# Gate rows by way of DRAM, one norm's row from an input, and x kept by the weights' queue, in a two-block transformer kernel

## The chip, the cores and the metric

The kernel runs on one core of a Trainium2 chip as one program. The metric is the device time of that program in microseconds. Its engines are named here as the profile does: PE is TensorE (PEld its weight loads), DVE VectorE, ACT ScalarE, POOL GpSimd, SP SyncE; SPq, POOLq and ACTq are the issuing of DMAs on those queues. The result must equal the reference in float32.

## What is computed

The reference runs two blocks of depth 2 on 256 tokens of width 1024. What touches the change:

```python
def rmsnorm(x, g):
    x32 = x.astype(jnp.float32)
    y = x32 * lax.rsqrt(jnp.mean(x32 * x32, axis=-1, keepdims=True) + EPS)
    return (y * g.astype(jnp.float32)).astype(x.dtype)
...
def first_block(x, c, ...):
    c_act = jax.nn.silu(c)
    for l in range(DEPTH):
        mod = c_act @ mod_w[l] + mod_b[l]
        sh1, sc1, g1, sh2, sc2, g2 = jnp.split(mod, 6, axis=-1)
        h = modulate(x, norm_g[l, 0], sh1, sc1)
        ...
        x = x + (g1[:, None, :] * y).astype(x.dtype)
        h = modulate(x, norm_g[l, 1], sh2, sc2)
        y = peer(h, peer_w_q[l], peer_subkeys[l], peer_u[l], peer_v[l])
        x = x + (g2[:, None, :] * y).astype(x.dtype)
        ...
    return rmsnorm(x, final_norm_g)

def second_block(x, c, ...):
    for layer in range(DEPTH):
        sh1, sc1, g1, sh2, sc2, g2 = jnp.split(c_act @ mod_w[layer] + mod_b[layer], 6, axis=-1)
        ...
        x = x + g1[:, None, :] * rms_norm(y, norm_g[layer, 1])
        h = modulate_2(rms_norm(x, norm_g[layer, 2]), sh2, sc2)
        y = sq_relu_mlp(h, ffn_w1[layer], ffn_w2[layer])
        x = x + g2[:, None, :] * rms_norm(y, norm_g[layer, 3])
    return x
```

`g2` is a vector of 1024 that multiplies every token's output, so on the chip it is wanted as a row repeated on all 128 partitions. `final_norm_g` is such a vector too.

## The kernel before

**Stages.** Block 1 runs a GLA mixer, PEER layer 0, sliding-window attention, PEER layer 1 and the final norm (`fin`). Block 2 runs an mLSTM mixer, FFN 0 (`f2_0`), MLA, and FFN 1 (`f2_1`). Tokens are two tiles of 128 (`NT`), the width eight chunks of 128 (`DC`) or two halves of 512.

**Weights.** A product in float32 is made of three products of halves: hi by hi, hi by lo, lo by hi. SP streams all weights as slabs of 1 MB into `ring`, two slabs deep, each slab in two transfers of 512 KB (L3198 for the first two slabs of a stage, L3214 in the loops, L3231 for the rest). ACT rounds a slab to its hi part (L1559), DVE makes the lo part (L1606), and PE multiplies. Before it loads into a half of `ring`, SP waits until that half's lo part is made.

**PEER.** A layer has a query stage (`peer_q`, L1459), scores of all 16384 experts (the u stage, 64 slabs), and the value loop (64 slabs, L2088, 24 products of 512 columns a slab). Between them GpSimd adds the chosen experts' weights into `routes` in DRAM by 128 indirect transfers (L1582). `routes` is cleared by SP in pieces of 1 MB (L3176); for layer 0 the last two pieces are issued behind the first and second slab of `peer_q0`.

**x kept.** The score inputs `h_parts` lie over the same memory as `x`. So GpSimd stores x to DRAM (`x_kept`, L3256, four transfers of 256 KB, each as soon as DVE has made that piece). In `peer_score_scalar` ACT waits for all four landings before `chunk_scalar` (L1025) writes `h_parts`. Near the end of the value loop GpSimd loads x back as `kept` (L3267, two transfers of 512 KB), for the residual.

**Gate rows.** modulation vectors are made as columns, `[128, 8]`, by DVE (`chunk_product`, L372) from strips that GpSimd loads: `first_mod_loads` before PEER layer 0, `strip_loads_gpsimd` (L411) in the value loops, `side_loads_gpsimd` (L452, four slots, each load waiting until the chunk four before it has been used) in the rest. `row_from_col` turns a column into a row on all partitions: DVE multiplies `ident` by the column (L473), and PE multiplies `ones` by the result into two PSUM banks (L484). `row_store` copies the banks to `row` (L492, DVE). `gated_vector` (L921) multiplies a stage's output by `row`. In each value loop the g2 row's products stand between slab 55 and 56, and in layer 1 those of the final norm's gain (`fin`) at slab 60. In the FFNs they stand behind the first step of the second matrix (`post_tensor`), and DVE copies them in `post_rest_vector`, behind the last split.

**Dummies.** `keep_busy_tensor` (L997) gives PE products of `ident` by itself, as many as the table `KEEP_BUSY` says, where it would wait; `pq0` is the place before the queries of PEER layer 0.

**Order.** The order of each engine is the order of the code; there is no planner. The queues are SP's (weights, clears), GpSimd's (strips, x kept, rows of c) and ACT's (routes' groups).

## Time and profile before

| | us |
|---|---|
| median of three runs | 2526.43 |
| the three runs | 2525.45, 2526.43, 2528.55 |
| the profiled execution's own time | 2524.33 |
| its span | 2522.6 |
| PE busy | 2448.2 (97%) |
| DVE busy | 2042.9 (81%) |
| ACT busy | 1266.6 (50%) |
| POOL busy | 672.4 (27%) |
| mean granted clock of TensorE | 0.989 |
| moved by DMA | 572.51 MB, mean 227 GB/s |

The span is from the first to the last instruction of the profiled execution; 1.7 us lie outside it. "Busy" is the share of the span in which an engine runs at least one instruction. A row of the timeline gives its start, how long it (or the group of like instructions) took, the engine and the line, the destination and the sources, and in brackets the idle time before it with what ended that.

### The profile page before, as it was taken

The page shows a single profiled execution, that of the slowest core. Times are in us where ns is not written, and L with a number is a line of the kernel's source. Part 1 is how long each engine was busy: PE and PEld are TensorE (multiplying, and loading weights), DVE is VectorE, ACT ScalarE, POOL GpSimd, SP SyncE. Part 2 cuts the span into 40 slices and gives each one's busy share as a digit, 9 for nine tenths or more (in the row PEclk, how much of TensorE's full clock was granted, in tenths as well). Part 3 has the DMA queues.
Part 4 walks back from the last instruction along what each step waited for, and adds up shares of the span by engine and source line. Part 5 has one row for each costly group of instructions (what it writes and reads, how often), then busy time and mean ns, then how long its engine had stood idle before and what let it go on. Part 6 is the DMA issues. An engine that isn't in the chain of part 4 may idle for free.

```text
span 2522.6 us, 41648 instructions
## 1 busy us (share of the span) xinstructions
PE 2448.2 (97%) x14618; PEld 2109.6 (84%) x14618; DVE 2042.9 (81%) x3772; ACT 1266.6 (50%) x1825; POOL 672.4 (27%) x548
## 2 busy tenths in 40 slices
PE   5999999999999999999999999999999999999998
PEld 4779988888888877899988888887878799867987
DVE  7888899888778888869999787778887887777754
ACT  5544555655444445445555555444454544334443
POOL 2113777772000001017777750001011000110000
PEclk8999999999999999999999999999999999999999
DMA  9976877776667987366777766668977567863554
GB/s 351 353 266 235 266 187 191 187 173 219 203 209 253 307 291 272 124 225 168 184 193 190 177 182 228 205 207 310 312 266 266 214 206 263 320 245 122 180 179 150
DMA packets 226199, 572.51 MB, mean 227 GB/s; under 512 B 55777, under 2 KB 86753, under 8 KB 225778
## 3 DMA queue, kind: packets, MB, share of 16 engines
q1 hardware_dynamic: 122674, 431.56, 50.6%
q0 software_dynamic: 70000, 120.43, 17.9%
q10 hardware_dynamic: 33360, 18.36, 2.4%
q8 instruction: 98, 1.61, 0.3%
q14 instruction: 67, 0.55, 0.1%
HBM read 550.20 MB, written 20.06 MB: 226 GB/s over the span
## 4 chain that ended last, share of the span: by engine, by line
PE 83%; DVE 9%; DMA 4%; ACT 3%; issue 2%; SPq 0%; POOL 0%; DVEq 0%; ACTq 0%; POOLq 0%
PE ps L2088 26%; PE ps L1526 14%; PE ps L1530 7%; PE ps L2829 7%; PE ps L744 6%; PE ps L1459 5%; PE ps L2811 5%; PE ps L1507 4%; PE ps L2815 2%; PE ps L1511 2%; DMA ring<-in_stream 2%; PE ps L1815 1%; ACT split_hi L1559 1%; DVE split_lo L1606 1%; DVE gate L921 1%
## 5 line engine op out<-in xcount | busy, mean ns | idle before, releaser
L1559 ACT ACTIVATE split_hi<-ring 128x1024 fp32r<-128x1024 f32 x760 | 800.6, 1056 | 678.0 <-PE ps L1530 222.5
L1606 DVE TENSOR_TENSOR split_lo<-ring,split_hi 128x1024 fp32r<-128x1024 f32 x676 | 823.4, 1219 | 177.8 <-ACT split_hi L1559 171.8
L1582 POOL DMA_INDIRECT routes<-small x256 | 478.1, 1868 | 162.4 <-issue 93.3
L1526 PE MATMUL ps<-h_parts,split_hi 128*128 128x512 f32 x1536 | 387.2, 394 | 0.2
L1526 PEld LDWEIGHTS ps<-h_parts,split_hi 128*128 128x128 f32 x1536 | 275.8, 189 | 49.9 <-issue 0.9
L1556 ACT ACTIVATE gate_hi<-gate 128x256 fp32r<-128x256 f32 x252 | 105.2, 418 | 369.1 <-PE ps L2088 357.6
L2088 PE MATMUL ps<-split_hi,gate_hi 128*128 128x512 f32 x1024 | 281.0, 394 | 2.1 <-DVE gate_lo L1604 1.3
L2088 PE MATMUL ps<-split_hi,gate_lo 128*128 128x512 f32 x1024 | 277.0, 390 | 4.6 <-DVE gate_lo L1604 4.4
L2088 PE MATMUL ps<-split_lo,gate_hi 128*128 128x512 f32 x1024 | 277.8, 391 | 0.0
L2088 PEld LDWEIGHTS ps<-split_hi,gate_lo 128*128 128x128 f32 x1024 | 191.4, 188 | 48.1 <-DVE gate_lo L1604 7.6
L2088 PEld LDWEIGHTS ps<-split_lo,gate_hi 128*128 128x128 f32 x1024 | 191.0, 188 | 44.9 <-DVE split_lo L1606 5.2
L2088 PEld LDWEIGHTS ps<-split_hi,gate_hi 128*128 128x128 f32 x1024 | 189.2, 188 | 43.1 <-ACT split_hi L1559 3.5
L1530 PEld LDWEIGHTS ps<-h_parts,split_lo 128*128 128x128 f32 x1536 | 209.2, 190 | 16.8 <-DVE split_lo L1606 2.1
L1530 PE MATMUL ps<-h_parts,split_lo 128*128 128x256 f32 x1536 | 214.4, 282 | 0.7 <-DVE split_lo L1606 0.7
L1604 DVE TENSOR_TENSOR gate_lo<-gate,gate_hi 128x256 fp32r<-128x256 f32 x252 | 106.4, 422 | 132.0 <-ACT split_hi L1559 131.9
L411 POOL DMA_DIRECT2D mod_w<-in_mod x64 | 34.0, 532 | 659.5 <-DVE strip_part L372 659.5
L452 POOL DMA_DIRECT2D small<-in_mod x104 | 55.2, 531 | 488.1 <-DVE modc L372 461.0
L372 DVE CUSTOM_DVE_ANT_0 small<-small,gate,cols 128x1024 f32<-128x1024 f32 x104 | 131.8, 1279 | 5.5 <-DMA small<-in_mod 5.5
L1507 PE MATMUL ps<-h_parts,split_hi 128*128 128x256 f32 x1024 | 133.7, 283 | 0.7 <-ACT split_hi L1559 0.6
L1507 PEld LDWEIGHTS ps<-h_parts,split_hi 128*128 128x128 f32 x1024 | 127.4, 192 | 1.2 <-ACT split_hi L1559 1.1
L2964 DVE TENSOR_TENSOR split_lo<-ring,split_hi 128x1024 fp32r<-128x1024 f32 x60 | 73.3, 1222 | 31.2 <-ACT split_hi L1559 31.2
L372 DVE CUSTOM_DVE_ANT_0 mod_w<-mod_w,c_loop 128x1024 f32<-128x1024 f32 x64 | 78.0, 1219 | 11.2 <-DMA mod_w<-in_mod 11.2
(412 smaller groups left out, 3739.2 us busy)
## 6 DMA issues: line engine op xcount, KB each, us to landing
ring<-in_stream SPq DMA_DIRECT2D x776, 512.0 KB, 4.8
small<-in_mod POOLq DMA_DIRECT2D x104, 512.0 KB, 5.9
mod_w<-in_mod POOLq DMA_DIRECT2D x64, 512.0 KB, 5.7
gate<-in_mod POOLq DMA_DIRECT2D x44, 512.0 KB, 6.9
routes<-u_part SPq DMA_DIRECT2D x16, 1024.0 KB, 12.8
small<-routes ACTq DMA_DIRECT2D x120, 128.0 KB, 5.4
gate<-in_mod SPq DMA_DIRECT2D x8, 512.0 KB, 16.1
routes<-small POOLq DMA_INDIRECT x256
```

Source lines behind the costliest of these rows:

```text
L372: return nc.vector.tensor_tensor_reduce(out=w, in0=w, in1=c_act, scale=1.0, scalar=start, op0=ALU.mult, op1=ALU.add, accum_out=out)
L744: return nc.tensor.matmul(ps[:, banks[2 * nb + i], :], src[:, b * per + n, i * P:(i + 1) * P], w[:, b % 2, at_:at_ + BANK], start=(b == n ...
L1459: ins = nc.tensor.matmul(out, w[:, b % 2, c * P:(c + 1) * P], src[:, c, :], start=(c == 0 and w is split_hi and src is hi), stop=(c == DC ...
L1507: nc.tensor.matmul(out, split_hi[:, e, c * P:(c + 1) * P], part[:, c, :], start=(part is hT_hi and c == 0), stop=False)
L1526: nc.tensor.matmul(ps[:, bank, :].rearrange("p (a n) -> p a n", a=2), split_hi[:, e, c * P:(c + 1) * P], h_parts[:, :, c, :], start=(c == ...
L1530: ins = nc.tensor.matmul(ps[:, bank, SEQ:2 * SEQ], split_lo[:, e, c * P:(c + 1) * P], hT_hi[:, c, :], start=False, stop=(c == DC - 1), ski ...
L1559: nc.scalar.activation(split_hi[:, e, :], ring[:, slot, e * D:(e + 1) * D], ACT.Copy).then_inc(hi_made, 1)
L1582: g.eng.indirect_dma_start(out=routes, out_offset=bass.IndirectOffsetOnAxis(ap=r_index[:, b, n:n + 1].bitcast(U32), axis=0), in_=r_weight[ ...
L1606: nc.vector.tensor_tensor(split_lo[:, e, :], ring[:, (START[name] + j) % RING, e * D:(e + 1) * D], split_hi[:, e, :].bitcast(F32), ALU.sub ...
L2088: return nc.tensor.matmul(ps[:, 2 * nb + n, :], g[:, e, n * P:(n + 1) * P], w[:, e, nb * BANK:(nb + 1) * BANK], start=opens, stop=True, sk ...
L2811: nc.tensor.matmul(out, split_hi[:, e, c * P:(c + 1) * P], part[:, c, :], start=(part is mlp_hi and c == 0), stop=False)
L2829: return nc.tensor.matmul(ps[:, 4 + 2 * nb + n, :], h[:, c0, n * P:(n + 1) * P], w[:, e, nb * BANK:(nb + 1) * BANK], start=(first and h is ...
```

## The change

Five of the rows are no longer made by products. For `g2_0`, `g2_1`, `f2_0` and `f2_1` GpSimd stores the column to DRAM (`gate_row_store`) and loads it back with the same 1024 values on every partition (`gate_row_load`). DVE waits for that landing in front of the residual. The row of `fin` is loaded in the same way from a new input. The rows of the mixers' gates are made as before.

GpSimd issues the g2 store behind the indirect adds, in front of the loads of the value loop's strips, and the row's load (in layer 1 also that of `fin`) behind the two loads of `kept`. In FFN 0 the store stands between side chunks 3 and 4, where GpSimd waits for the gain column, and the load in front of side chunk 7. For FFN 1 both stand behind all side loads.

The stores of x to `x_kept` go from GpSimd's queue to SP's, behind the first two slabs of `peer_q0` and `peer_q1` and, in layer 0, behind the two clears. `KEEP_BUSY["pq0"]` goes from 12 to 2.

SP at the start of PEER layer 0 before (L3198 are the halves of `peer_q0`'s first two slabs, L3176 the clears, L3214 the slab loop):

```order
L3198 DMA ring<-in_stream 128x1024 x2
L3176 DMA routes<-u_part 512x1x512
L3198 DMA ring<-in_stream 128x1024 x2
L3176 DMA routes<-u_part 512x1x512
L3226 UNCONDITIONAL_BRANCH
L3226 ISA
L3214 ISA
L3214 DMA ring<-in_stream 128x1024
```

and now:

```order
L3204 DMA ring<-in_stream 128x1024 x2
L3182 DMA routes<-u_part 512x1x512
L3204 DMA ring<-in_stream 128x1024 x2
L3182 DMA routes<-u_part 512x1x512
L3217 DMA x_kept<-x 128x512 x4
L3238 UNCONDITIONAL_BRANCH
L3238 ISA
L3226 ISA
L3226 DMA ring<-in_stream 128x1024
```

The four stores of x stand behind the second clear on SP's queue.

GpSimd from the end of the value loop of layer 0 to the strips of layer 1's before (L3267 is `kept`, L334 the next block's or stage's row of c, L452 the side chunks, L3256 x kept, L1569 the first splits of the u stage, L1582 the indirect adds, L1590 the first groups of routes):

```order
L3267 DMA gate<-x_kept 128x1024 x2
L334 DMA gate<-c_kept 128x1024
L452 DMA small<-in_mod 128x1024 x16
L3256 DMA x_kept<-x 128x512 x4
L452 DMA small<-in_mod 128x1024 x8
L1569 TENSOR_TENSOR split_lo<-ring,split_hi 128x1024 x12
L1582 DMA routes<-small 2097152x1 x128
L1590 DMA small<-routes 128x2x128 x4
L337 DMA c_loop<-c_kept 128x1024
```

and now (L507 is the row's load, L501 the column's store):

```order
L3280 DMA gate<-x_kept 128x1024 x2
L507 DMA gate<-gate_rows 128x1024
L336 DMA gate<-c_kept 128x1024
L456 DMA small<-in_mod 128x1024 x24
L1586 TENSOR_TENSOR split_lo<-ring,split_hi 128x1024 x12
L1599 DMA routes<-small 2097152x1 x128
L1607 DMA small<-routes 128x2x128 x4
L501 DMA gate_rows<-modc 128x8x1
L339 DMA c_loop<-c_kept 128x1024
```

The row's load stands behind `kept`, the column's store behind the indirect adds, and the side chunks no longer have the stores of x among them.

PE at the end of the value loop of layer 0 before:

```order
L2088 MATMUL ps<-split_lo,gate_hi 128x512 x4
L2117 REGISTER_ALU
L2117 COMPARE_AND_BRANCH
L484 MATMUL ps<-gate,ones 128x512 x2
L2088 MATMUL ps<-split_hi,gate_hi 128x512 x4
L2088 MATMUL ps<-split_hi,gate_lo 128x512 x4
```

and now:

```order
L2092 MATMUL ps<-split_lo,gate_hi 128x512 x4
L2121 REGISTER_ALU
L2121 COMPARE_AND_BRANCH
L2092 MATMUL ps<-split_hi,gate_hi 128x512 x4
L2092 MATMUL ps<-split_hi,gate_lo 128x512 x4
```

The two products of ones behind the loop's branch are gone.

The diff, cut:

```diff
         x_kept, x_back = sem("x_kept"), sem("x_back")
+        gate_row_stored, gate_row_landed, fin_row_landed = sem("gate_row_stored"), sem("gate_row_landed"), sem("fin_row_landed")
+        GATE_ROWS = ["g2_0", "g2_1", "f2_0", "f2_1"]
         sems = {"V": vector_steps, "A": scalar_steps, "T": tensor_steps, "G": gpsimd_steps, "S": slab_used, "L": lo_free}
...
-        def side_loads_gpsimd(g, stage, first=0, last=None):
-
-            for s in SIDE_STRIPS[stage][first:last]:
+        def side_loads_gpsimd(g, stage, first=0, last=None, between=()):
+
+            for q, s in enumerate(SIDE_STRIPS[stage][first:last]):
                 for k in range(DC):
                     n = SIDE.index(s) * DC + k
+                    if (q, k) in between:
+                        between[q, k]()
                     if n >= 4:
...
                     .then_inc(vector_steps, v.step(f"{name}.row{n}"))
+
+        def gate_row_store(eng, name, col):
+            n = GATE_ROWS.index(name)
+            eng.dma_start(io["gate_rows"][n].rearrange("(c p) -> p c", p=P), col,
+                          allow_slow_non_contiguous=True).then_inc(gate_row_stored, 16)
+
+        def gate_row_load(eng, name):
+            n = GATE_ROWS.index(name)
+            eng.wait_ge(gate_row_stored, 16 * (n + 1))
+            eng.dma_start(row[:, :], io["gate_rows"][n].partition_broadcast(P)).then_inc(gate_row_landed, 16)
+
+        def gate_row_wait(eng, name):
+            eng.wait_ge(gate_row_landed, 16 * (GATE_ROWS.index(name) + 1))
...
         KEEP_BUSY = {"n2_0": 14, "n1_1": 16, "n2_1": 13, "m1": 32, "m2_0": 22, "m1_1": 21, "m2_1": 21,
-                     "swa.q": 13, "ml.h": 11, "pq0": 12,}
+                     "swa.q": 13, "ml.h": 11, "pq0": 2}
...
                     strip_part_vector(v, l, slab // 8, slab % 8)
-                if slab == 31:
-                    v.eng.wait_ge(lo_free, TILE0[f"v{l}"] + 2 + LAYER // SEQ)
-                    if l == 0:
-                        first_strip_made(v, G2)
-                    row_from_col(v, f"g2_{l}", modc[:, PLACE[MOD1[l] + G2], :], 5, "V")
-                if slab == 57:
-                    row_store(v, f"g2_{l}", 5)
-                if l and slab == 58:
-                    row_from_col(v, "fin", col("fin"), 5, "V")
-                if l and slab == 61:
-                    row_store(v, "fin", 5, fin_row)
             v.seen.clear()
...
                         routes_group_tensor(t, (2 * l + 1) * GROUPS + 4 * i + j // 2)
-                    if l and isinstance(i, int) and (i, j) == (7, 4):
-                        row_from_col(t, "fin", None, 5, "T")
                     if isinstance(i, int) and i == j == 7:
...
             t.seen.clear()
-            row_from_col(t, f"g2_{l}", None, 5, "T")
             body(7)
...
             v.eng.wait_ge(strip_stored, (l + 1) * LOOP_STRIPS + 1)
+            gate_row_wait(v.eng, f"g2_{l}")
             tile_residual_vector(v, f"peer{l}.res", ("n1_1", "fin")[l], (1, 0)[l], returned=l + 1)
...
                     .then_inc(vector_steps, v.step(f"fin.x{i}{nb}"))
+            v.eng.wait_ge(fin_row_landed, 16)
             scaled(0, 0)
...
                 side_strip_made(v, g)
-            nc.vector.tensor_tensor(scale_c2[:, :], modc[:, PLACE[g], :], gain, ALU.mult).then_inc(vector_steps, v.step())
-            row_from_col(v, f"{name}.g", scale_c2[:, :], row_bank, "V")
-
-        def post_rest_vector(v, name, row_bank, bank, norm):
-            row_store(v, f"{name}.g", row_bank)
+            nc.vector.tensor_tensor(scale_c2[:, :], modc[:, PLACE[g], :], gain, ALU.mult) \
+                .then_inc(vector_steps, v.step(f"{name}.gain"))
+            if row_bank is not None:
+                row_from_col(v, f"{name}.g", scale_c2[:, :], row_bank, "V")
+
+        def post_rest_vector(v, name, bank, norm):
+            gate_row_wait(v.eng, name)
             v.wait_ge(vector_steps, v.n)
...
             free[0] = free[1] = free[2] = free[3] = []
-            post_tensor(t, f"f2_{l}", 0)
             for i in range(1, MLP_STEPS):
...
             less_splits_vector(v, f"ffn1_{l}", 1, 2)
-            post_gain_vector(v, f"f2_{l}", col("norm2", 4 * l + 3), MOD2[l] + G2, 0)
+            post_gain_vector(v, f"f2_{l}", col("norm2", 4 * l + 3), MOD2[l] + G2, None)
...
             ffn2_less_vector(v, l, 2, FF // P)
-            post_rest_vector(v, f"f2_{l}", 0, 4, ("m1_1", None)[l])
+            post_rest_vector(v, f"f2_{l}", 4, ("m1_1", None)[l])
...
                         clear_routes(0, 6 + s - a)
+                for l in range(2):
+                    if a == START[f"peer_q{l}"]:
+                        for i in range(NT):
+                            for nb in range(2):
+                                sp.wait_ge(*when(f"{('gla_out', 'swa_out')[l]}.x{i}{nb}"))
+                                sp.dma_start(io["x_kept"][:, i, half(nb)], x[:, i, half(nb)]).then_inc(x_kept, 16)
                 if a == START["qa"]:
...
             for l in range(2):
-                for i in range(NT):
-                    for nb in range(2):
-                        g.wait_ge(*when(f"{('gla_out', 'swa_out')[l]}.x{i}{nb}"))
-                        pool.dma_start(io["x_kept"][:, i, half(nb)], x[:, i, half(nb)]).then_inc(x_kept, 16)
                 if l:
...
                 routes_gpsimd(g, l)
+                if l:
+                    g.wait_ge(*when(f"side{SIDE.index(MOD1[1] + G2) * DC + DC - 1}"))
+                else:
+                    pool.wait_ge(first_mod_used, FIRST_CHUNKS + (G2 - 1) * DC)
+                gate_row_store(pool, f"g2_{l}", modc[:, PLACE[MOD1[l] + G2], :])
                 strip_loads_gpsimd(pool, l)
...
                     pool.dma_start(kept[:, i, :], io["x_kept"][:, i, :]).then_inc(x_back, 16)
+                gate_row_load(pool, f"g2_{l}")
+                if l:
+                    pool.dma_start(fin_row, io["fin"].partition_broadcast(P)).then_inc(fin_row_landed, 16)
                 g.wait_ge(*when(f"peer{l}.full"))
...
             pool.dma_start(dkv_w, io["dkv"][:, :]).then_inc(dkv_landed, 16)
-            for l in range(2):
-                side_loads_gpsimd(g, ("ff_0", "mla")[l])
+            def f2_0_store():
+                g.wait_ge(*when("f2_0.gain"))
+                gate_row_store(pool, "f2_0", scale_c2[:, :])
+            side_loads_gpsimd(g, "ff_0", between={(0, 4): f2_0_store, (0, 7): lambda: gate_row_load(pool, "f2_0")})
+            side_loads_gpsimd(g, "mla")
+            g.wait_ge(*when("f2_1.gain"))
+            gate_row_store(pool, "f2_1", scale_c2[:, :])
+            gate_row_load(pool, "f2_1")
...
         "qb_rope": c(chunked(np.ascontiguousarray(qb[:, [0, 4, 1, 5, 2, 6, 3, 7], NOPE:]).reshape(LORA_Q, -1)).reshape(P, -1)),
-        "stream": stream, "mod": c(mod), "cols": c(colv), "rows": rowv,
+        "fin": c(g["final_norm_g"].reshape(D)), "stream": stream, "mod": c(mod), "cols": c(colv), "rows": rowv,
         "c_rows": c(np.stack([g["c"].reshape(D), g["c_2"].reshape(D)])), "pos": c(pos).astype(np.int32),
...
         io["out"] = nc.dram_tensor("out_x", (P, NT, D), F32, kind="ExternalOutput").ap()
+        io["gate_rows"] = nc.dram_tensor("gate_rows", (4, D), F32, kind="Internal").ap()
         io["c_kept"] = nc.dram_tensor("c_kept", (2, D), F32, kind="Internal").ap()
...
         io["x_kept"] = nc.dram_tensor("x_kept", (P, NT, D), F32, kind="Internal").ap()

```

## Rows read from the trace of the kernel before

**Rows 1.** The page, the chain that ended last: shares of the span.

```profile
PE 83%; DVE 9%; DMA 4%; ACT 3%; issue 2%; SPq 0%; POOL 0%; DVEq 0%; ACTq 0%; POOLq 0%
```

**Rows 2.** Timeline (start us, us, ...), PE, end of layer 0's value loop.

```profile
917.19 1.88 PE L484 MATMUL ps<-gate,ones 128*128 128x512 f32 x4
918.50 1.50 PE L2088 MATMUL ps<-split_hi,gate_hi 128*128 128x512 f32 x4
919.84 1.08 PE L2088 MATMUL ps<-split_hi,gate_lo 128*128 128x512 f32 x4
920.76 1.08 PE L2088 MATMUL ps<-split_lo,gate_hi 128*128 128x512 f32 x4
```

**Rows 3.** Timeline, DVE and PE, near the end of layer 1's value loop.

```profile
1839.11 1.28 DVE L492 COPY gate<-ps 128x512 f32<-128x512 f32 x2
...
1842.25 1.20 PE L2088 MATMUL ps<-split_lo,gate_hi 128*128 128x512 f32 x4
```

**Rows 4.** Timeline, start of PEER layer 0: POOL, PE, ACT, PE.

```profile
159.25 0.69 POOL L3256 DMA_DIRECT2D x_kept<-x  x1 [0.78 <-DVE stat L913]
...
161.44 1.09 PE L1009 MATMUL ps<-ident,gate 128*128 128x128 f32 x8 [0.47 <-DVE gate L982]
...
166.40 3.76 ACT L1025 ACTIVATE h_parts<-ps,modc,scale_c 128x256 fp32r<-128x256 f32 x8 [4.78 <-DMA x_kept<-x]
...
167.10 3.69 PE L1459 MATMUL ps<-h_parts,split_hi 128*128 128x256 f32 x8 [1.90 <-ACT h_parts L1025]
```

**Rows 5.** SP's issues at 149 to 153, with ns and landings.

```profile
L3198 SPq DMA_DIRECT2D ring<-in_stream x2: 328/328/328, 149.9 to 152.5; - x2
...
DMA to landing us min/median/max: 14.2/14.2/14.2
L3176 SPq DMA_DIRECT2D routes<-u_part x1: 570/570/570, 152.8 to 152.8; - x1
...
DMA to landing us min/median/max: 15.7/15.7/15.7
```

**Rows 6.** Windows: us, PE, PEld, DVE, ACT, POOL busy, PEclk, DMA share, GB/s.

```profile
161.00:165.00 4.00, 3.56 (x32) 3.56 (x32) 1.68 (x3) 0.62 (x1) 0.00 (x0) 1.00 1.02 416
169.00:175.80 6.80, 6.80 (x29) 6.23 (x30) 6.80 (x16) 3.16 (x5) 0.32 (x1) 0.50 0.08 22
```

**Rows 7.** Timeline, start of PEER layer 1: PE, ACT.

```profile
1079.46 1.09 PE L1009 MATMUL ps<-ident,gate 128*128 128x128 f32 x8 [0.47 <-DVE gate L982]
...
1080.54 1.48 ACT L1025 ACTIVATE h_parts<-ps,modc,scale_c 128x256 fp32r<-128x256 f32 x3 [0.89 <-DMA x_kept<-x]
```

**Rows 8.** Tails of both loops: a window, ACT, the `kept` loads, DVE.

```profile
952.00:958.00 6.00, 6.00 (x28) 4.99 (x27) 4.67 (x9) 2.85 (x5) 0.00 (x0) 1.00 1.02 404
...
1868.80 1.06 ACT L1559 ACTIVATE split_hi<-ring 128x1024 fp32r<-128x1024 f32 x1 [0.94 <-DMA ring<-in_stream]
...
L3267 POOL DMA_DIRECT2D gate<-x_kept x2: 531/531/531, 1859.3 to 1859.8; - x2
...
DMA to landing us min/median/max: 7.9/10.1/12.3
...
1874.49 0.69 DVE L921 TENSOR_TENSOR gate<-ps,gate 128x512 f32<-128x512 f32 x1 [0.59 <-PE ps L2088]
```

**Rows 9.** POOL's adds and gap, DVE's columns, and side loads (page).

```profile
562.64 1.95 POOL L1582 DMA_INDIRECT routes<-small  x1 [4.19 <-issue]
564.89 1.90 POOL L1582 DMA_INDIRECT routes<-small  x1 [0.30 <-issue]
...
2027.98 0.16 DVE L2521 TENSOR_TENSOR scale_c<-modc,cols 128x8 f32<-128x8 f32 x1
...
2052.51 0.53 POOL L452 DMA_DIRECT2D small<-in_mod  x1 [44.99 <-DVE modc L372]
...
2073.91 1.28 DVE L372 CUSTOM_DVE_ANT_0 small<-small,gate,cols 128x1024 f32<-128x1024 f32 x1
...
small<-in_mod POOLq DMA_DIRECT2D x104, 512.0 KB, 5.9
```

## The prediction

> **What bounds the kernel now.** I read the chain of waits first: 83% of the span hangs on TensorE, 9% on VectorE, 4% on a transfer [rows 1]. So a product removed from TensorE's stream in a loop counts in full, a VectorE copy counts only where TensorE waits for VectorE, and a transfer counts at the few places where its landing ends a wait. The timeline by engine then shows the places that the change touches: the end of the PEER value loop, where the products of ones stand between value products [rows 2]; a row's copies from PSUM beside the loop's splits [rows 3]; the start of PEER layer 0, where ScalarE waits 4.78 us for the last `x_kept` store [rows 4] while the transfers issued around it take 14 to 16 us [rows 5]; TensorE's granted clock there [rows 6]; the same place in layer 1, almost without a wait [rows 7]; the loop tails, where the transfer engines are full [rows 8]; and GpSimd's gaps, where the new store has to fit [rows 9].
>
> **The sum's base.** The profiled execution took 2524.33 us, of which 2522.6 us are the span. It is 2.1 us under the median of the three runs. Terms are read in it and taken from the median.
>
> **Term 1, the products of ones.** In layer 0 the two products (four records, since each row of the moving matrix goes through more than once) start at 917.19 and the four hi-hi products behind them at 918.50; the hi-lo products start at 919.84, and the four of them last to 920.76, so four such products cost 0.92 [rows 2]. Without the products of ones the hi-lo products would start 919.84 - 917.19 - 0.92 = 1.73 us earlier. The rows of layer 1, of the two FFNs and of the final norm are the same two products with the same shapes. TensorE's rows on both sides have no idle time before them. Five rows by 1.72: **-8.6 us**. Bounds: 5 x 1.31 = 6.5 (the distance from 917.19 to 918.50 alone) and 5 x 1.88 = 9.4.
>
> **Term 2, VectorE's part.** Of each row go a product of `ident` with the column and two copies, 1.28 us for both copies [rows 3]. VectorE has room in most of the loop, but behind the copies the splits come late: the group of four lo-hi products at 1842.25 lasts 1.20 instead of 1.08 and starts later than the rhythm asks [rows 2, 3]. Taking 0.12 for each of four such places in the value loops gives **-0.5**. Bounds 0 and -1.5 (one whole copy of 0.64 us at two places, and 0.2). In the FFN the copies stood at the very end of the loop, hidden by the last products: nothing.
>
> **Term 3, x kept in layer 0.** `h_parts` lies over `x`, so ScalarE's L1025 may not write before all four stores landed. Before, they are issued on GpSimd's queue up to 159.25 and ScalarE starts at 166.40, after 4.78 us of idle time, though the second turn, which it also needs, began at 161.44 [rows 4]. So the floor is 161.6, a gain of 4.8. The change gives the stores to SP's queue, where two ring halves and a clear of `routes` of 1 MB have just been issued. The ring halves took 14.2 us to land and the clear, issued at 152.8, took 15.7: it ends at 168.5 [rows 5]. The transfer engines are full (share 1.02 in the window from 161 [rows 6]), so the total of bytes ends at about 168.5 in either order. If SP's queue works in order, the clear comes first and the stores last: they land at about 168.5, ScalarE starts at 168.6: **+2.2 us**. The last store of 256 KB at 416 GB/s is another 0.6: +2.8 at worst. If they overtake, -4.8. I take +2.2, since the ring halves behind the first clear are the nearest row, and their 14.2 us show a transfer of this same queue held up by a clear ahead of it.
>
> Here a rule of the Trainium skill speaks against any effect of the queue. The page "DMA: Bandwidth & Descriptors", section "Rules for kernel authors", says that issuing from another engine gives no bandwidth, because all of them run on the same 16 engines and interleave. By that the stores would land where they do now, and term 3 would be 0. That is a rival below.
>
> **Term 4, the clock and the dummies there.** Ten of the twelve dummy products go; the product behind them waits 1.90 us for ScalarE, until 167.10, so they are under the wait: 0 by themselves [rows 4]. But TensorE's pause grows from 1.9 us to about 6 us. From 169.0 to 175.8 the granted clock is 0.50 already now, which is 1.2 GHz instead of 2.4, behind the pause of 1.9 us [rows 6]. TensorE is busy for all of these 6.8 us, so they would be at most 3.4 us shorter at the full clock. I take **0**, and half of that either way for the range, since the splits on the two other engines don't follow the clock: +-1.7.
>
> **Term 5, x kept in layer 1.** ScalarE idles 0.89 us for the last store and starts at 1080.54; the turn it also needs began at 1079.46, so some of the 0.89 stays [rows 7]. On SP's queue there is no clear ahead in this layer, and the stores are issued as each tile is ready: **-0.5** (0 to -0.9).
>
> **Term 6, the tails of the value loops.** Behind the two `kept` loads now stands a broadcast load of 512 KB (layer 0), two of them in layer 1, while the last ring slabs come in. The transfer engines are full here (1.02 at 404 GB/s [rows 8]), so each 0.524 MB at 404 GB/s takes 1.3 us of them. The ring is already felt: ScalarE waits 0.94 us for a half at 1868.80, and the `kept` loads, issued at 1859.3 and 1859.8, take up to 12.3 us, to 1872.1, against 1874.49 when VectorE needs the row (L921) [rows 8]. If all of it were passed on: 1.3 + 2.6 = 3.9, and about 1 more where VectorE waits for the row itself. What is queued behind the wait on VectorE is the whole residual, and TensorE's next turns behind that. Against it: most of the load falls after the last ring half has been issued, and `fin` is needed only about 5 us after the row. I take **+0.8**, a fifth; bounds 0 and +4.9.
>
> **Term 7, the stores of the columns.** Each takes 1024 elements of 4 bytes from [128, 8] to DRAM on GpSimd. No row shows such a store. From below: a plain transfer's issue, 0.53 us [rows 9]. From above: an indirect one of 128 elements takes 1.95 us behind 4.19 of GpSimd's own, the following ones 1.90 behind 0.30 [rows 9]; eight times the first is 49 us, eight times the others 17.6. In FFN 0, the tightest place, VectorE makes the gain column at 2027.98 to 2028.14, and GpSimd is idle for 44.99 us until 2052.51, when it issues side chunk 4, used at 2073.91 [rows 9]; such a load takes 5.9 us [rows 9]. So the cover is 24.3 us of idle time and 15.5 of lead, 39.8 us. In the PEER layers the loads behind the store are for strips of the loop's second half, and for f2_1 nothing follows: **0**.
>
> The same page and section state that a transfer with a non-contiguous last dimension becomes one descriptor per element. It would make this store 1024 descriptors; the trace cannot tell, and the bounds above allow for it.
>
> **Sum:** -8.6 - 0.5 + 2.2 + 0 - 0.5 + 0.8 + 0 = **-6.6 us**, 2526.4 - 6.6 = **2519.8 us**.
>
> **The rivals.**
> A, *the stores overtake*: SP's stores are taken up beside the clear and land before 162. For: SP issues them as each tile is ready, from 155. Against: four stores of 1 MB need 2.6 us of full engines, and 14.2 us for ring halves in the same queue. Term 3 is -4.8 instead of +2.2: -13.6, **2512.8**; with the clock gain 2511.1. 12%.
> B, *no effect of the queue*: the rule above; the mechanism here is that the stores share the full engines with clear and halves in equal parts whoever issued them, and land at 166.4 as now. Term 3 is 0: -8.8, **2517.6**. 14%.
> C, *the tails are passed on*: the ring halves of the last slabs come late by the added transfers. For: the 0.94 us wait that is there already. Term 6 is +3.9 to +4.9 instead of +0.8: -3.5 to -2.5, about **2523.4**. 18%.
> D, *slower*: the column store in FFN 0 keeps GpSimd for longer than its cover. At the upper bound chunk 4 is issued at 2028.2 + 49 = 2077.2 and lands at 2083.1, 9.2 us after VectorE wants it; VectorE's splits stand behind it, TensorE behind those. -6.6 + 9.2 = +2.6, **2529.0**. It makes the change a loss from a store of 46.4 us on. Against: the steady 2.2 us for 128 elements. 3%.
> E, *nothing comes out*: the products of ones filled gaps that open again. Against: no idle time stands by the products next to them. Term 1 halves: **2524.1**. 3%.
> The forecast itself has 50%, its own range 2517.5 to 2522.
>
> **Range and chances.** The range reaches to A and over C: **2511.5 to 2525.0**. 0.2%, about what a measurement of this kernel can tell from no change, is 5.05 us, so faster means under 2521.4. The forecast gives 42 of its 50 there, A 12, B 12: **0.66**. Slower, over 2531.5: D with a longer store, or several bounds together: **0.04**. Within: **0.30**.
>
> **What would show it.** Term 1: the first value product behind the loop's branch follows without the 1.7 us. Term 3: ScalarE's L1025 in layer 0 starts at 168.6 and waits for `x_kept`; at 162 A is right, at 166.4 B. Term 4: the windows after it at 0.50 for no longer than now. Term 5: in layer 1 no wait for `x_kept`. Term 6: the wait for the ring in the last slabs under 1 us and none of L921 for the row. Term 7: GpSimd's store issue under 40 us. The forecast is wrong if the layer 0 start moves by more than 3 us, or if a tail loses more than a product row gained.

## The result and the profile after

The changed kernel takes 2529.75 us (median of 19 runs, 2521.24 to 2540.01), the kernel before on the same chips 2524.37 us (19 runs, 2519.10 to 2529.78). The ratio is 1.0022, with a 95% interval of 1.0012 to 1.0033: it is slower by 5.4 us, and certainly not faster. The forecast was 2519.8 us and a range of 2511.5 to 2525.0; both are missed, and the sign with them. The tables and rows below come from one profiled execution of each kernel: that of after took 2526.96 us, 2.8 under its median, that of before 2524.33.

The page of the changed kernel: span, PE's busy time, and the chain that ended last.

```profile
span 2525.0 us, 41558 instructions
PE 2436.0 (96%) x14578; PEld 2103.1 (83%) x14578; DVE 2031.0 (80%) x3757; ACT 1266.1 (50%) x1825; POOL 675.0 (27%) x549
PE 79%; DVE 10%; DMA 6%; ACT 3%; issue 2%; SPq 0%; POOL 0%; DVEq 0%; ACTq 0%; POOLq 0%
```

PE is busy for 12.2 us less than before (2448.2), of which 2.2 are dummy products (40.8 to 38.6 us) that ran under a wait; DVE is busy for 11.9 less: the work went as meant. But the chain's share of transfers rose from 4% [rows 1] to 6%. The view of waits says which: ACT waiting for a slab. First the two rows of after (us in total, times, longest), then the one of before.

```profile
ACT split_hi L1576 <- DMA ring<-in_stream: 49.4, 23, 7.0
...
ACT split_hi L1699 <- DMA ring<-in_stream: 7.9, 2, 5.4
```

```profile
ACT split_hi L1559 <- DMA ring<-in_stream: 29.5, 16, 4.5
```

So ACT waits 27.8 us more for the ring; what of it reaches the end is another matter, since PE goes on with what lies ready. ACT issues the same 1674 activations in the same order in every kernel of this study, so the start of the k-th of them in one run less its start in the run of before tells where time goes. This table is worked out from the timelines so; its columns are us of offset against the profiled execution of before.

```
start in before, and what it is         after  a_rows32  a_xpool  a_turned
 121.39  before PEER layer 0             0.70    -0.34     -1.13    -0.17
 166.40  ACT L1025, x_kept landed        3.71     2.48     -0.76     0.17
 273.27  scores of layer 0               1.50     1.16     -1.50    -1.23
 591.51  end of the scores, layer 0      1.56     0.68     -1.19    -1.11
 605.20  first slabs of the value loop   6.43     0.68     -1.19    -1.11
 891.61  value loop, ahead of row           6.06     0.29     -1.37    -1.82
 921.88  behind the row's products       3.49    -2.23     -3.69    -3.25
 948.05  26 us behind those              1.98    -3.29     -4.31    -4.50
 966.65  behind the loop                 3.22    -2.17     -3.71    -4.47
1481.11  scores of layer 1               1.01     3.40     -5.40    -4.64
1760.19  value loop, layer 1             2.23     3.81     -3.47    -4.36
1861.75  its tail                       -2.30    -0.67     -7.83    -8.18
1877.33  behind the loop                -1.25     0.16     -8.49    -7.99
2036.35  FFN 0                           1.60     1.17     -8.21    -7.03
2042.11  FFN 0, 6 us on                  4.46     1.17     -4.46    -7.03
2148.73  behind the row's products       2.19    -0.55     -5.26    -8.64
2343.51  FFN 1                           0.71    -2.03     -5.29   -10.11
2351.19  FFN 1, 8 us on                  4.13    -2.03     -2.86   -10.11
2455.90  behind the row's products       2.42    -3.75     -4.57   -11.72
2516.81  the last activation             2.44    -3.72     -4.55   -11.69
```

The column of after climbs at four places, by 4.9, 1.2, 2.9 and 3.4 us, **12.4 us in all**: each is a few us behind one of the four column stores. (The third is read before it has settled: from 2044.02 on it is 3.90, and 11.8 of the 12.4 stay.) a_xpool, which has the same stores, climbs by 0, 1.5, 3.8 and 2.4 us there (the third settles at 4.7): whether a stop becomes a wait seems to depend on what the ring holds just then. At its first store the last halves of the ring had been issued from 584.4, 2.8 us earlier than in after. The column falls where the products of ones stood. Steps of 1 to 5 us elsewhere stand where the kernels don't differ, as at the start or in the attention between 966 and 1481 (a_rows32 +5.6, a_turned -0.2). There is one profile of each kernel, so I can't trace them; the unprofiled runs of before alone spread over 10.7 us. For the same reason the last row is not the difference of the medians: after ends at +2.4 where the medians say +5.4, and a_rows32, whose profiled execution (2520.51) was the slowest of its nine, at -3.7 where they say -8.8.

The first two places in the timeline of after: ACT at the start of the value loop of layer 0, and in FFN 0.

```profile
602.15 1.06 ACT L1699 ACTIVATE split_hi<-ring 128x1024 fp32r<-128x1024 f32 x1 [5.42 <-DMA ring<-in_stream]
...
2044.35 1.06 ACT L1576 ACTIVATE split_hi<-ring 128x1024 fp32r<-128x1024 f32 x1 [5.82 <-DMA ring<-in_stream]
```

At 2038.26 before, the same activation waited 1.33 us for PE. GpSimd's four stores of the columns in after (issue in ns, then the landing of all four):

```profile
L501 POOL DMA_DIRECT2D gate_rows<-modc x2: 919/923/927, 585.4 to 1495.6; - x2
L501 POOL DMA_DIRECT2D gate_rows<-scale_c x2: 911/912/913, 2028.5 to 2336.3; - x2
...
DMA to landing us min/median/max: 11.0/11.2/11.8
```

GpSimd is done with each in 0.92 us, near the lower bound of my term 7 (0.53); but the transfer of 4 KB lands only 11 us later. What it does to the others meanwhile: the ring halves issued from 587 to 591, who waited for them, and their landing.

```profile
L3204 SPq DMA_DIRECT2D ring<-in_stream x2: 339/339/339, 587.2 to 589.3; - x2
...
  ACT split_hi L1699: 5.4, 1
...
DMA to landing us min/median/max: 14.1/14.5/15.0
```

The three ring halves of 2028 to 2034 in after land after 10.5 us in the median, up to 14.2; in before after 4.8. The windows (us, busy PE, PEld, DVE, ACT, POOL, PEclk, DMA share, GB/s), first after, then before:

```profile
590.00:597.00 7.00, 7.00 (x58) 6.30 (x57) 6.11 (x10) 3.88 (x5) 0.00 (x0) 1.00 0.36 16
2032.00:2040.00 8.00, 8.00 (x69) 8.00 (x68) 5.97 (x8) 3.37 (x5) 0.00 (x0) 1.00 0.57 16
```

```profile
590.00:597.00 7.00, 7.00 (x53) 6.17 (x52) 5.99 (x9) 3.76 (x5) 0.00 (x0) 1.00 0.52 178
2032.00:2040.00 8.00, 8.00 (x69) 8.00 (x68) 6.25 (x9) 3.67 (x4) 0.00 (x0) 1.00 0.72 215
```

For seven and eight microseconds all transfers together move 16 GB/s, where before they moved 178 and 215. The busy share of the transfer engines falls too (0.36 against 0.52, 0.57 against 0.72); the trace doesn't show what holds them. Behind the two other stores, at 1495.6 and 2336.3, it is the same for six and four microseconds:

```profile
1499.60:1505.60 6.00, 6.00 (x50) 5.30 (x48) 5.11 (x8) 3.24 (x4) 0.00 (x0) 1.00 0.44 17
2340.30:2344.30 4.00, 4.00 (x35) 4.00 (x35) 2.37 (x4) 2.11 (x3) 0.00 (x0) 1.00 0.88 27
```

PE is still busy in all of them, on what the ring holds. ACT's waits begin at 596.7 and 2038.5, some 7 us after the flow has stopped, when that is used up. This is why no engine's own row names the store.

The other steps of the prediction in after's timeline: PEER layer 0 (SP's four stores of x in one row, then ACT, then PE), and ACT in layer 1.

```profile
156.01 4.63 SPq L3217 DMA_DIRECT2D x_kept<-x  x4
...
170.11 3.76 ACT L1042 ACTIVATE h_parts<-ps,modc,scale_c 128x256 fp32r<-128x256 f32 x8 [7.49 <-DMA x_kept<-x]
...
170.81 3.68 PE L1476 MATMUL ps<-h_parts,split_hi 128*128 128x256 f32 x8 [6.83 <-ACT h_parts L1042]
...
1082.05 1.47 ACT L1042 ACTIVATE h_parts<-ps,modc,scale_c 128x256 fp32r<-128x256 f32 x3 [0.38 <-PE ps L1026]
```

Against [rows 4] the wait grew from 4.78 to 7.49 us; against [rows 7] the 0.89 us for `x_kept` in layer 1 are gone and ACT waits for PE. In the tails, where [rows 8] have one wait of 0.94 for the ring:

```profile
962.42 1.06 ACT L1576 ACTIVATE split_hi<-ring 128x1024 fp32r<-128x1024 f32 x1 [1.06 <-DMA ring<-in_stream]
...
1867.14 1.06 ACT L1576 ACTIVATE split_hi<-ring 128x1024 fp32r<-128x1024 f32 x1 [1.83 <-DMA ring<-in_stream]
...
1869.89 1.06 ACT L1576 ACTIVATE split_hi<-ring 128x1024 fp32r<-128x1024 f32 x1 [1.39 <-DMA ring<-in_stream]
...
1873.23 0.69 DVE L938 TENSOR_TENSOR gate<-ps,gate 128x512 f32<-128x512 f32 x1 [0.61 <-PE ps L2092]
```

### The profile page after: what moved, and what is told of

Its sections match the earlier page's. It is cut to its first block, busy times and chain, and to the rows that moved or that the text cites. A ratio compares the mean times of both kernels' runs of the same rounds, so it can differ in the third digit from the quotient of the medians.

```text
span 2525.0 us, 41558 instructions
## 1 busy us (share of the span) xinstructions
PE 2436.0 (96%) x14578; PEld 2103.1 (83%) x14578; DVE 2031.0 (80%) x3757; ACT 1266.1 (50%) x1825; POOL 675.0 (27%) x549
## 4 chain that ended last, share of the span: by engine, by line
PE 79%; DVE 10%; DMA 6%; ACT 3%; issue 2%; SPq 0%; POOL 0%; DVEq 0%; ACTq 0%; POOLq 0%
PE ps L2092 26%; PE ps L1543 13%; PE ps L2836 7%; PE ps L1547 7%; PE ps L761 6%; PE ps L1476 5%; DMA ring<-in_stream 4%; PE ps L2818 4%; PE ps L1524 3%; PE ps L2822 2%; PE ps L1528 2%; DVE split_lo L1623 1%; ACT split_hi L1576 1%; PE ps L1832 1%; DVE gate L938 1%
```

## The experiments

Theory S: an element-wise store to 4 KB of DRAM holds up the other transfers, and the ring runs dry behind it. Its rivals: it is the place or the queue of the store (Q), or the row loads and the moved stores of x (P).

### The same store in pieces of 32 bytes, and the stores alone

a_rows32, against the changed kernel:

```diff
-            eng.dma_start(io["gate_rows"][n].rearrange("(c p) -> p c", p=P), col,
-                          allow_slow_non_contiguous=True).then_inc(gate_row_stored, 16)
+            eng.dma_start(io["gate_rows"][n].rearrange("(p c) -> p c", p=P), col).then_inc(gate_row_stored, 16)
```

> The changed kernel, but each of the four columns is stored as 128 pieces of 32 bytes instead of 1024 of 4 bytes; the order of the values in the gate rows is then wrong (the part of the computation that changes), the transfers, waits and sizes are the same. Theory S (the element-wise store holds all 16 transfer engines for about 9 us and the weight ring runs dry): in the four places behind a store, ScalarE's waits for the ring of 3 to 5.5 us go, about 12 us in all against the changed kernel; the kernel is faster than before by 7 to 12 us. Theory Q (a store on GpSimd's queue at that place is what hurts, whatever its pieces): the waits stay, and the time is that of the changed kernel within 2 us.

2514.42 us, ratio to before 0.9972 (0.9960 to 0.9983), where the changed kernel has 1.0022: 0.50% or 12.6 us less. Q is out. The four steps of the offset are gone (table), and ACT's waits for the ring are 35.8 us in all, where after has 57.3 and before 29.5. The store in FFN 0 now lands in 3.6 us:

```profile
L501 POOL DMA_DIRECT2D gate_rows<-scale_c x1: 548/548/548, 2029.6 to 2029.6; - x1
...
DMA to landing us min/median/max: 3.6/3.6/3.6
```

b_store, against the kernel before (at the four places the change has them; nobody reads the result):

```diff
+        def gate_row_store(eng, n, col):
+            eng.dma_start(io["gate_rows"][n].rearrange("(c p) -> p c", p=P), col,
+                          allow_slow_non_contiguous=True).then_inc(gate_row_stored, 16)
...
                 routes_gpsimd(g, l)
+                gate_row_store(pool, l, modc[:, PLACE[MOD1[l] + G2], :])
...
+            side_loads_gpsimd(g, "ff_0", between={(0, 4): f2_0_store})
```

> The kernel before with the four column stores alone added at their places, nothing reads them; rows are still made by products. Theory S: +10 to +14 us against before, with late ring halves behind each store (peaks of about 5, 2, 5 and 5 us in the offset). Theory P (the loss comes from the loads of the rows or the moved x stores, not from the stores): within 1.5 us of before.

2541.51 us, ratio 1.0075 (1.0049 to 1.0100): +18 us, more than expected. P is out. In the profiled execution, which ends at +18.1, the offset rises by 2.2, 2.1, 5.9 and 4.9 us behind the four stores, 15.1 us; between them some 4 are given back, and 7.0 stand in the offset already at 121.39, before the first store, where the kernels don't differ. Only four runs carry this median; I read it as 11 us (18.1 less 7.0) to 18 us by the stores, and the 7.0 stay unexplained.

### The stores of x

a_xpool, against the changed kernel: the loop of four `x_kept` stores is taken out of SP's block and put back at the head of the loop over the layers in GpSimd's.

> The changed kernel with the stores of x back on GpSimd's queue, at their old places. If SP's queue holds them behind the second clear: ScalarE's start in PEER layer 0 comes about 2.7 us earlier than in the changed kernel, its wait is about 4.8 us instead of 7.5, and in layer 1 about 0.9 us of wait comes back: in all -1.5 to -3 us. If the queue makes no difference: 0, with the 7.5 us wait still there.

2524.70 us, ratio 1.0009 (0.9996 to 1.0022), 3.3 us under the changed kernel's ratio; the two intervals overlap, so the sum is weak, but the row is plain:

```profile
165.63 3.76 ACT L1042 ACTIVATE h_parts<-ps,modc,scale_c 128x256 fp32r<-128x256 f32 x8 [5.16 <-DMA x_kept<-x]
```

The wait is 5.16 us instead of 7.49: here the queue matters. Of the 2.6 us by which after falls behind a_xpool between 121 and 166, 1.2 are left at 273 (after 1.50 - 0.70, a_xpool -1.50 + 1.13).

a_clears, against the changed kernel:

```diff
-                    if a == START["peer_q0"]:
-                        clear_routes(0, 6 + s - a)
                 for l in range(2):
                     if a == START[f"peer_q{l}"]:
...
+                if a == START["peer_q0"]:
+                    clear_routes(0, 6)
+                    clear_routes(0, 7)
```

> The changed kernel, but in layer 0 the two clears of routes are issued behind the stores of x on SP's queue instead of ahead of them. If SP's queue works in order: ScalarE's wait for x_kept in PEER layer 0 goes from 7.5 to under 1.5 us, its start is 6 to 7 us earlier; the clears then lie beside the query slabs and may give 0 to 4 us back: -2 to -7 us against the changed kernel. If the transfers share the engines whatever the order: the wait stays above 4 us.

2521.62 us, ratio 0.9990 (0.9981 to 0.9999): 8 us under the changed kernel, one more than the expected range. In the profile 5.0 of them stand at ACT's start in PEER layer 0 (offset -1.33 where after has 3.71); the rest isn't traced. b_clears is the same edit on the kernel before, with the stores of x moved to SP:

> The kernel before with the stores of x on SP's queue and the two clears behind them; rows by products and 12 dummies as before. Against before: ScalarE's start in PEER layer 0 4 us earlier, layer 1 0.5 to 0.9 us earlier, less what the clears cost beside the query slabs: -1 to -5 us. If the clears are passed on in full: 0.

2519.53 us, ratio 0.9985 (0.9975 to 0.9994): -4 us, by the other queue and the order together. ACT's row in layer 0, first of a_clears, then of b_clears:

```profile
165.07 3.76 ACT L1042 ACTIVATE h_parts<-ps,modc,scale_c 128x256 fp32r<-128x256 f32 x8 [2.97 <-DMA x_kept<-x]
```

```profile
163.08 3.76 ACT L1025 ACTIVATE h_parts<-ps,modc,scale_c 128x256 fp32r<-128x256 f32 x8 [2.88 <-DMA x_kept<-x]
```

The wait is 7.49 us with the clears ahead, 2.97 with the clears behind, not under 1.5 as I had written. Between after and a_clears the queue and the bytes are the same and only the order differs, so what is issued first on SP's queue is served first here. What the remaining 2.97 us are no run shows; the ring halves ahead and GpSimd's strips beside are my guess.

### The final norm's row alone

b_fin, against the kernel before: the two products and two copies of `fin` go, and GpSimd loads `fin_row` from the input behind `kept`.

> The kernel before with only the final norm's row loaded from an input: -1.7 us from the two products and about -0.5 from VectorE's work, less what 512 KB more in the tail of layer 1's value loop costs (0 to 1.3 us): -1 to -2.5 us. If the transfer in the tail is passed on in full: 0.

2522.27 us, ratio 0.9999 (0.9986 to 1.0011): nothing to be told. In its profiled execution the expected step is not there: DVE waited 2.71 us for a strip load just at that place (1848.87), and PE 2.46 us behind it. One execution doesn't tell whether that belongs to the edit.

### The element-wise store cut in time, and spread in space

a_spread, against a_xpool: each store becomes eight, one column each, one for every slab used.

```diff
+            for k in range(DC):
+                if pace is not None:
+                    eng.wait_ge(lo_free, pace + 2 * k)
+                if only is None or only == k:
+                    eng.dma_start(io["gate_rows"][n].rearrange("(c p) -> p c", p=P)[:, k:k + 1], col[:, k:k + 1],
+                                  allow_slow_non_contiguous=True).then_inc(gate_row_stored, 16)
```

> The kernel a_xpool (x stored by GpSimd's queue) with each element-wise store cut into eight of 128 elements, one for every slab used (5.8 us apart). Theory S with a ring that covers short stops: each piece holds the transfer engines for an eighth of 11 us, 1.4 us, less than the ring's lead, so no late ring half is left behind the stores: 10 to 14 us under a_xpool, 8 to 12 us under the kernel before. If the held time counts in full however it is cut: no change against a_xpool.

2587.06 us, ratio 1.0253 (1.0239 to 1.0266): +63 us where I expected -10. Both alternatives had the held time in proportion to the elements, and that is what fell. It is the stores and not their spacing: ACT's waits for the ring are 162.2 us in 62 places (a_xpool 45.3 in 23), while DVE waits 8.1 us for the strips issued behind the stores (a_xpool 8.4). The four of them issued from 2062 to 2100:

```profile
L505 POOL DMA_DIRECT2D gate_rows<-scale_c x4: 548/548/551, 2062.4 to 2099.9; - x4
...
DMA to landing us min/median/max: 9.8/12.2/17.2
```

128 elements, 512 neighbouring bytes, take as long as 1024 elements over 4 KB. A new theory was needed. Theory L: small elements cost little by themselves (N would have it otherwise); the stop comes when several transfer engines write into the same small piece of DRAM at once. By this theory one column is the worst case.

b_store_wide, against b_store:

```diff
-            eng.dma_start(io["gate_rows"][n].rearrange("(c p) -> p c", p=P), col,
+            eng.dma_start(io["gate_rows"][n].rearrange("(c p) w -> p c w", p=P)[:, :, 0], col,
                           allow_slow_non_contiguous=True).then_inc(gate_row_stored, 16)
...
-        io["gate_rows"] = nc.dram_tensor("gate_rows", (4, D), F32, kind="Internal").ap()
+        io["gate_rows"] = nc.dram_tensor("gate_rows", (4, D, P), F32, kind="Internal").ap()
```

> The kernel b_store (before, with the four element-wise column stores that nothing reads), but each of the 1024 elements of 4 bytes goes to a place of its own, 512 bytes from the next, in a larger DRAM tensor. Theory N (each small element costs the transfer engines its time, wherever it goes): the stalls and the +18 us of b_store stay. Theory L (the cost is that all 16 engines write elements into the same few hundred bytes of DRAM at once): the stalls go and the time is within 4 us of before.

2526.27 us, ratio 1.0006 (0.9993 to 1.0020), against 1.0075 of b_store. b_store_64 is the same with `(4, D, 16)`, elements 64 bytes apart:

> The kernel b_store with the elements 64 bytes apart in DRAM instead of 4 (b_store: +18 us against before) or 512 (b_store_wide: +1.6 us and no separate stall). If elements of different engines disturb each other only within 64 bytes: no stall, within 4 us of before. If it is within a larger piece of DRAM that holds several of these places: late ring halves behind the stores come back, +5 to +18 us.

2524.06 us, ratio 1.0001 (0.9990 to 1.0011). The landings of all four stores in b_store, b_store_wide and b_store_64:

```profile
DMA to landing us min/median/max: 10.4/11.4/11.7
```

```profile
DMA to landing us min/median/max: 4.6/4.8/5.9
```

```profile
DMA to landing us min/median/max: 4.4/5.0/6.6
```

The same 1024 elements, the same queue, the same places: 4 bytes apart they cost 11 to 18 us, 64 bytes apart nothing that can be measured. N falls: the distance in DRAM decides. The other half of L, that several engines must write there at once, is argued and not shown: no run sent neighbouring elements through one engine. What inside the memory or the engines makes it so, the runs don't say either.

### The versions that beat both

a_turned, against a_xpool: PE turns the column `[128, 8]` by one small product, DVE copies 8 rows of 128, GpSimd stores those behind the strips, and the row is loaded as in the change. Place and pieces of the store both differ from a_xpool, so a_rows32 above stays the clean test of the pieces.

```diff
+                nc.tensor.transpose(ps[0:DC, bank, 0:P], diag[:, 0, 0:DC], ident[:, :]) \
+                    .then_inc(tensor_steps, t.step(f"{name}.turn"))
...
+                nc.vector.tensor_copy(row[0:DC, 0:P], ps[0:DC, bank, 0:P]) \
+                    .then_inc(vector_steps, v.step(f"{name}.flat"))
...
+            g.eng.dma_start(io["gate_rows"][n].rearrange("(c p) -> c p", p=P), row[0:DC, 0:P]) \
+                .then_inc(gate_row_stored, 16)
```

> The kernel a_xpool with the column turned by one small TensorE product into 8 rows of 128 values, copied by VectorE and stored as 8 pieces of 512 bytes; everything is computed. Theory S: the stalls go and a small product (about 0.3 us) and two small copies a row come back: 9 to 12 us under a_xpool, 7 to 11 us under the kernel before. If it is the way through DRAM at all that costs, as a_xpool.

2513.34 us, ratio 0.9959 (0.9946 to 0.9972); ACT waits 30.2 us for the ring, as before (29.5). PE at the place of [rows 2]:

```profile
914.65 1.07 PE L2119 MATMUL ps<-split_lo,gate_hi 128*128 128x512 f32 x4
915.55 0.27 PE L509 MATMUL ps<-ident,gate 128*8 128x128 f32 x1
915.58 1.17 PE L2119 MATMUL ps<-split_hi,gate_hi 128*128 128x512 f32 x4
916.59 1.08 PE L2119 MATMUL ps<-split_hi,gate_lo 128*128 128x512 f32 x4
```

From the start of the hi-hi products to the hi-lo ones it is 1.01 us where 0.91 is usual: the turn costs 0.1 us, where the two products of ones cost 1.73.

a_clears_turned has both mends:

> The changed kernel with both mends: the column turned by a small product and stored as 8 pieces of 512 bytes, and the two clears of routes behind the stores of x on SP's queue. Everything is computed. If the two effects add: a_turned's 11 us under before and another 1 to 3 us from PEER layer 0 and 1: 2510 to 2513 us. If the moved clears only shift the wait: as a_turned.

2509.35 us, ratio 0.9952 (0.9935 to 0.9969), 1 us below the expected range; the interval overlaps that of a_turned, so what the moved clears add is not told by the times. And a_turned_kb12 is that with `"pq0": 12` again:

> a_clears_turned with the 12 dummy products ahead of the queries of PEER layer 0 instead of 2. If the dummies hold the clock: the stretch at the low clock behind ScalarE's wait falls from about 7 us to about 3.5, up to 1.8 us faster. If they are covered by the wait and the clock falls anyway: no difference, or up to 1 us slower where they end behind ScalarE's start.

2508.52 us, ratio 0.9949 (0.9931 to 0.9967). The two don't differ measurably; both are some 12 to 15 us under the kernel before. The windows from 165 to 170, a_clears_turned and then a_turned_kb12:

```profile
165.00:170.00 5.00, 4.79 (x22) 4.20 (x23) 5.00 (x14) 2.47 (x5) 0.00 (x0) 0.69 0.50 200
```

```profile
165.00:170.00 5.00, 4.20 (x23) 3.13 (x24) 5.00 (x15) 2.72 (x6) 0.00 (x0) 1.00 0.46 182
```

With 12 dummies and a wait of 2.9 us the clock stayed at 2.4 GHz, with 2 of them it was at 1.2 GHz for part of that window; ACT's offset gains 1.5 us from 166.40 to 177.08 with 12 (-3.45 to -4.99), 0.9 with 2 (-3.92 to -4.86). But b_clears, also with 12 dummies and a wait of 2.9 us, has the clock down too:

```profile
165.00:170.00 5.00, 4.67 (x18) 3.86 (x19) 5.00 (x16) 2.78 (x6) 0.00 (x0) 0.67 0.48 190
```

So whether the dummies hold the clock stays open; the cut from 12 to 2 bought nothing that can be measured.

## Why the prediction was wrong, step by step

**Term 1, the products: right.** In the FFNs the offset falls by 1.70 and 1.71 us where they stood (2135.78 to 2148.73, 2440.19 to 2455.90; forecast 1.72 each), in the value loops by 1.80 and 1.77 at the g2 rows (5.29 at 898.32 to 3.49 at 921.88, 1.02 at 1816.99 to -0.75 at 1832.37), and by 1.34 at the place of `fin` (1843.48 to 1856.31).

**Term 2, DVE: within its bounds, as far as it can be told.** From 898.32 to 945.37 and from 1816.99 to 1856.31 the offset falls by 3.29 and 3.34 us, 1.5 more than three rows of 1.72. By the same reckoning it is 1.4 in a_rows32 and 0.4 in a_xpool; I took 0.5, with 1.5 as the bound. That it is VectorE's relief is argued from its removed rows, not isolated by a run. The larger falls in the table don't all belong to it: the 1.3 us at 1764.64 in layer 1 are there in b_fin, b_clears, b_store and both wide stores too (0.9 to 1.4), which still make the g2 row by products. It is a wait of the profiled execution of before:

```profile
1760.32 1.23 DVE L372 CUSTOM_DVE_ANT_0 mod_w<-mod_w,c_loop 128x1024 f32<-128x1024 f32 x1 [1.78 <-DMA mod_w<-in_mod]
```

**Term 3, x kept in layer 0: right in its mechanism and place, too small there.** ACT's wait grew by 2.7 us (7.49 against 4.78), and its start came at 170.11 instead of 168.6: 3.7 us later than before, of which 0.7 stood in the offset already. That is at my upper bound of 2.8 and just meets my own sign of being wrong, a start moved by more than 3 us. The clear landed at 167.5 (153.8 + 13.7), and the last store of x only 2.6 us behind it, where I had both land together; that the stores wait behind the clear a_clears shows. Rival B, the sharing of engines in equal parts, would have left 4.8 us and is out, and so is the early landing of A. The rule named beside B, of the Trainium skill, "DMA: Bandwidth & Descriptors", section "Rules for kernel authors", speaks of bandwidth, and the trace agrees: from 160 to 165 it is 415 GB/s, before 416. The rule doesn't say who is served first within one queue. About 1.2 us of the loss were left 100 us later.

**Term 4, the clock: no price to be seen.** No run isolates it; from 166.40 to 177.08 the offset falls by 1.0 us, it doesn't rise. After the longer pause the low clock lasted longer: the granted clock in the five-us windows from 165 on is 0.70, 0.50 and 0.78.

```profile
165.00:170.00 5.00, 0.00 (x0) 0.00 (x0) 0.00 (x0) 0.00 (x0) 0.00 (x0) 0.70 0.98 383
170.00:175.00 5.00, 4.18 (x12) 3.10 (x13) 3.77 (x12) 4.70 (x9) 0.00 (x0) 0.50 0.01 6
175.00:180.00 5.00, 5.00 (x35) 5.00 (x35) 5.00 (x10) 1.27 (x2) 0.53 (x1) 0.78 0.20 56
```

That is 3.0 + 5.0 + 2.2 = 10.2 us at 1.2 GHz against some 7 before, but 3 of them lie in the pause itself.

**Term 5: right** (the wait for `x_kept` is gone), too small to be seen in the sum.

**Term 6, the tails: inside its bounds.** From 948.05 to 966.65 and from 1861.75 to 1877.33 the offset rises by 1.2 us in layer 0 and 1.1 in layer 1, 2.3 in all where I took 0.8, with bounds of 0 and 4.9. But a_turned, with the same loads of rows, has 0.0 and 0.2 there, and a_xpool 0.6 and -0.7: how much the loads cost is not shown. DVE never waited for a row in after, and rival C's 3.9 to 4.9 us didn't come.

**Term 7, the column stores: this is the step that failed.** I took 0 and measured **12.4 us** in the profile and 12.6 between the ratios of after and a_rows32. With it the forecast's sum of -6.6 becomes +6.0; measured are +5.4. That they meet so closely is in part luck, given the misses of terms 3 and 6 and steps of some us that no edit explains. The error was not a size but a place: I bounded how long GpSimd would be held (0.53 to 49 us; it was 0.92) and compared that with GpSimd's idle time, 39.8 us. Nothing in the working asked what the transfer does to the other transfers on the same 16 engines, above all to the ring, which ran dry some 7 us after the flow had stopped. Rival D had the right instruction and the wrong resource: its point of decision, 46.4 us of issue, was never near, while the loss was there at 0.92.

I had also cited the rule for this very edit, and let it stand as something the bounds allow for. The Trainium skill, "DMA: Bandwidth & Descriptors", section "Rules for kernel authors", advises to rearrange so that the last dimension is contiguous; a_turned does that, and is 11 us faster than the kernel before. The same page's section "Specifications" says that a transfer below 512 bytes is done by read-modify-write. The runs here agree that small neighbouring writes can be dear, but they show that size is not enough: pieces of 32 bytes side by side (a_rows32), and of 4 bytes at a distance of 64 (b_store_64), cost nothing measurable.

## What to carry to other kernels

Price a transfer by what it does to the other transfers in flight, not by the engine that issues it: look for the stream that runs beside it, and for how many microseconds that stream's buffers last. A column that is to become a row in DRAM is first turned on TensorE (0.1 us here) and stored as a few long pieces. Within one queue, order is time: what an engine waits for is issued ahead of a large transfer that nobody waits for (with two clears of 1 MB behind instead of ahead, the wait was 2.97 us instead of 7.49).

## What the runs showed of the hardware

- A store of 4 KB as 1024 elements of 4 bytes, side by side in DRAM, landed after 11 us, and for 4 to 8 of them all transfers together moved 16 to 27 GB/s, where in the two windows compared they moved 178 and 215 before. With the elements 64 or 512 bytes apart it landed after about 5 us and the weight stream ran on.
- The time doesn't go with the number of elements: 128 of them in 512 neighbouring bytes landed after 9.8 to 17.2 us. 32 such stores cost about 62 us more than the four of 1024 in a_xpool, 2 us each; four of 1024 cost 12.6 against a_rows32, 3 us each.
- In and behind a pause of 6.8 us of TensorE the granted clock was 1.2 GHz for about 10 us, some 3 of them in the pause, against some 7 behind the pause of 1.90 us [rows 4] of before. Twelve dummy products ahead of a shorter wait kept it at 2.4 GHz in one kernel (a_turned_kb12) and not in another (b_clears).
